# The recurrent stage of a hybrid decoder step: powers, exponentials and keys in another order

## The reference

```python
def rwkv7_scan(r, decay, k, v, kk, kka, s0):
    def step(s, inp):
        r_t, w_t, k_t, v_t, kk_t, kka_t = inp
        s_kk = jnp.einsum('bhvk,bhk->bhv', s, kk_t)
        s = s * w_t[:, :, None, :] - s_kk[..., None] * kka_t[:, :, None, :] + v_t[..., None] * k_t[:, :, None, :]
        return s, jnp.einsum('bhvk,bhk->bhv', s, r_t)
...
    w_log = -jax.nn.softplus(-(w0 + jnp.tanh(zw) @ w2).astype(f32)) - 0.5
    decay = jnp.exp(-jnp.exp(w_log))
    a = jax.nn.sigmoid((a0 + za @ a2).astype(f32))
...
    kk = k * ph(k_k)
    kk = kk / jnp.maximum(jnp.sqrt(jnp.sum(kk * kk, axis=-1, keepdims=True)), 1e-12)
    k = k * (1.0 + (a - 1.0) * ph(k_a))
    y, s_final = rwkv7_scan(r, decay, k, v, kk, kk * a, s0.astype(f32))
```

## Time and profile before

| what | value |
|---|---|
| median of 3 runs | 3446.24 us (3445.89 to 3452.47) |
| profiled execution, its own time | 3446.67 us |
| its span, first to last instruction | 3445.1 us |
| mean granted TensorE clock | 0.952 |
| TensorE matmuls busy | 3162.6 us (92%) |
| VectorE busy | 2162.1 us (63%) |
| ScalarE busy | 1105.0 us (32%) |
| GpSimd busy | 521.5 us (15%) |

### The profile page before, as it was taken

The page is one execution under the profiler, slowest core; times in us unless marked ns, Lnnn a source line. Parts: engine busy times, 40 slices in busy tenths (PEclk is TensorE's granted clock), DMA queues, the critical chain, the costliest instruction groups (busy, mean ns, idle before and its releaser), DMA issues. The chain is left out here.

```text
span 3445.1 us, 66198 instructions
## 1 busy us (share of the span) xinstructions
PE 3162.6 (92%) x25784; PEld 1917.1 (56%) x25784; DVE 2162.1 (63%) x4342; ACT 1105.0 (32%) x2313; POOL 521.5 (15%) x732
## 2 busy tenths in 40 slices
PE   8999999999999999869999865877876999999998
PEld 4544445555555555446666544777765555555553
DVE  2017889999999999658776554677772444432221
ACT  4135660000000000135555324677762211111221
POOL 3331000000000000021111132455542000000000
PEclk9999999999999999979999976889897999999999
DMA  5232111111111111132111181222215211221110
GB/s 161 72 93 66 43 41 57 56 55 58 55 57 62 55 58 55 59 96 67 43 44 33 49 271 47 57 62 66 64 31 158 100 52 54 64 78 58 49 40 25
DMA packets 215817, 233.54 MB, mean 68 GB/s; under 512 B 28665, under 2 KB 191028, under 8 KB 215012
## 3 DMA queue, kind: packets, MB, share of 16 engines
q1 hardware_dynamic: 147960, 110.07, 11.8%
q0 software_dynamic: 23696, 59.79, 6.0%
q10 hardware_dynamic: 43868, 59.62, 5.0%
HBM read 158.75 MB, written 70.63 MB: 67 GB/s over the span
## 5 line engine op out<-in xcount | busy, mean ns | idle before, releaser
L409 PE MATMUL fro_acc<-h_t,fro_w 128*128 128x416 f32 x3280 | 1174.6, 516 | 0.0
L409 PEld LDWEIGHTS fro_acc<-h_t,fro_w 128*128 128x128 f32 x3280 | 614.5, 190 | 543.1 <-issue 536.1
L692 DVE TENSOR_SCALAR_CACHE_REDUCE fro_work<-scores,fro_real 128x384 uint8<-128x384 f32 (+6 forms) x462 | 656.2, 1474 | 2.1
L516 ACT ACTIVATE fro_out<-fro_acc 128x416 f32<-128x416 f32 (+3 forms) x230 | 118.0, 513 | 794.1 <-PE fro_acc L409 711.6
L3105 DVE CUSTOM_DVE_ANT_0 att_seen<-att_ps,scores 128x512 f32<-128x512 f32 (+3 forms) x320 | 181.4, 608 | 99.8 <-PE att_ps L2991 99.5
L2169 PE MATMUL mrg_po<-mrg_wo,mrg_mrg 128*128 128x512 f32 (+1 forms) x544 | 238.8, 597 | 4.6 <-DVE mrg_mrg L2274 4.6
L2201 PE MATMUL mrg_pg<-mrg_wg,mrg_x_t 128*128 128x512 f32 (+1 forms) x544 | 236.3, 592 | 0.0
L658 DVE SCALAR_TENSOR_TENSOR scores<-fro_work,w_idx,scores 128x512 f32<-128x512 f32 (+3 forms) x280 | 188.0, 671 | 39.2 <-ACT fro_work L573 12.2
L3075 ACT ACTIVATE att_seen<-att_seen,att_shift 128x128 f32<-128x128 f32 (+15 forms) x128 | 152.6, 1194 | 83.2 <-DVE att_shift L3113 83.2
L2169 PEld LDWEIGHTS mrg_po<-mrg_wo,mrg_mrg 128*128 128x128 f32 (+1 forms) x544 | 101.5, 187 | 139.1 <-issue 134.1
L573 ACT ACTIVATE fro_work<-fro_wk 128x512 f32<-128x512 f32 (+3 forms) x320 | 144.5, 540 | 90.7 <-PE fro_wk L482 89.8
(11 more groups left out here) (449 smaller groups left out, 4523.5 us busy)
## 6 DMA issues: line engine op xcount, KB each, us to landing
z_t<-fro_out ACTq DMA_DIRECT2D x180, 208.0 KB
fro_w<-in_w_in SPq DMA_DIRECT2D x41, 512.0 KB, 4.1
mrg_m_in<-z_t POOLq DMA_DIRECT2D x56, 256.0 KB, 3.5
scores<-in_cache_kv POOLq DMA_DIRECT2D x108, 128.0 KB, 3.1
rwk_zi<-z_t SPq DMA_DIRECT2D x80, 129.0 KB, 2.6
z_t<-fro_out ACTq DMA_DIRECT2D x45, 192.0 KB
scores<-in_x_prompt SPq DMA_DIRECT2D x16, 512.0 KB, 8.4
mrg_x<-in_x_prompt SPq DMA_DIRECT2D x16, 512.0 KB, 3.5
```

Source lines behind the costliest of these rows:

```text
L409: last = pe.matmul(acc[e % 2][:, 0:CW], w[block_no % 3][:, kk, :], h_t[:, kk, CW * g:CW * g + CW], start=(kk == 0), stop=(kk == KD - 1))
L692: chain.mark(dve.tensor_scalar(junk[b % 2][:, 0:n], scores[:, c:c + n], realf[:, b:b + 1], None, op, ALU.add, accum_out=count[:, b:b + 1]))
```

## The change

Only the order of calls inside a round changes, on three engines. No instruction is added or taken away, and GpSimd's and SyncE's lists stay as they are.

```diff
@@ TensorE
                 if inverse:
                     square(n + 1, 2)
-                if features:
-                    norms(n + 2)
                 if loop:
                     take_in(n, 1)
                 if inverse:
                     square(n + 1, 3)
+                if features:
+                    norms(n + 2)
+                if inverse:
                     turn_rates(n + 1)
@@ ScalarE
                 if norm:
                     deviation(n - 1)
+                if inverse:
+                    take_square(n + 1, 1)
                 if features:
                     exps(n + 2)
+                if inverse:
+                    take_keys(n + 1)
+                    take_square(n + 1, 2)
+                if features:
                     spread_norms(n + 2)
                     take_values(n + 2)
-                if inverse:
-                    take_square(n + 1, 1)
-                    take_keys(n + 1)
-                if features:
                     key_mix(n + 2)
-                if inverse:
-                    take_square(n + 1, 2)
@@ VectorE
                 if loop:
                     next_state(n, 1)
+                if inverse:
+                    power(n + 1, 3)
                 if features:
                     unit_key(n + 2)
                     mixed_key(n + 2)
-                if inverse:
-                    power(n + 1, 3)
                 if inputs:
                     add_parts(n + 3, 1)
-                if features:
-                    scaled_keys(n + 2)
                 if inverse:
                     power(n + 1, 4)
                 if features:
+                    scaled_keys(n + 2)
                     scaled_rows(n + 2)
```

## The result

| | median | range | runs |
|---|---|---|---|
| before | 3449.22 us | 3445.89 to 3452.47 | 4 |
| after | 3501.53 us | 3499.45 to 3514.28 | 4 |

The ratio is 1.016 with a 95% interval of 1.014 to 1.0181: 52 us slower, where 35 were forecast. The direction was right, the time lies 7.5 us above the end of the range. The profiled execution of the changed kernel took 3514.28 us, 13 more than its median and 67.6 more than the profiled one before. Of these 67.6 us, 55.9 lie in rounds 0 to 12 of the recurrent stage, 3.9 in its other rounds, and 7.8 outside the stage, where the two kernels are the same. So part of the 13 us is scatter of other stages.

What follows compares the result with a forecast made beforehand. The recurrent stage was taken as bound by a chain from engine to engine, no engine full. Longer rounds 28.3, other rounds 0.7 and tail clock 6.5 made 35.5 us on 3446.67, giving 3481 us, range 3460 to 3494.

Steps and rivals of the forecast that it cites:

- Edit 1, the cancellation: ScalarE's second-power copy ahead of the exponentials: 2.25 us earlier, but the third-power copy starts when it does today.
- Edit 2, the inputs later: VectorE's unit and mixed keys behind power 3: next inputs (L1740) end 1.40 us later, round 31.59 us.
- the collision: VectorE's L1739 beside GpSimd's L1204: the stretching moves to L1740 or L1204, -0.2 to +0.3 us a round.
- Edit 3: VectorE's scaled keys behind power 4: 1.14 us out of power 4's way, gain covered; costs nothing by 0.3 us.
- Size (a), square 1 slow in five rounds: TensorE's square 1 at the 1.2 GHz level in five of 13 rounds: 0.83 us more in those, mean 31.91.
- Size (b), the clock in the tail: TensorE at the lower clock behind new idle late in the round: 1.0 us in half the rounds, bounds 0 and 1.0.
- The path: ScalarE's squash of the next inputs (L1525): whatever moves it moves the round, 4.85 us before the next.
- the bonus arm: GpSimd's product, then TensorE's bonus sums and side: side ready at 2391.6, wanted by ScalarE only at 2393.38.
- The other rounds: The filling round and round 13 of the recurrent stage: together 0.7 us more, bounds -1.4 and +1.4.
- TensorE's faster square 2: Rival: square 2 at full clock without its idle, round's end following TensorE: 10 us less, 3436; 7 in 100.
- the tail had no give: Rival denied here: 1.4 to 2 us of give in ScalarE's tail absorbs the later L1740, 3440 to 3453; 7 in 100.

Runs made afterwards that it cites:

- Edit 1 alone: Kernel before with only ScalarE's second power copied ahead of the exponentials and the third ahead of norms, values and key mix: 3444.93 us, ratio 0.9978.
- the filled hole: Kernel before with ScalarE copying values and spreading norms while square 1 runs, then copying the second power, then the exponentials: 3430.19 us, ratio 0.9935.
- edit 2 alone: Kernel before with only VectorE's power 3 moved ahead of the unit and mixed keys: 3530.83 us, ratio 1.0235.
- The filled gaps: Changed kernel with 4 extra TensorE matmuls ahead of square 4 and 16 ahead of the bonus sums, results unused: 3480.19 us, ratio 1.008.

## Why the forecast was right in kind and short in size

- **Edit 1, the cancellation: right.** Behind square 1's copy there are 8.41 us to the last power copy (8.48 forecast), with no idle. Edit 1 alone gave 6 us, close to nothing, and the filled hole bears the reading out: with 0.99 us less behind the copy, the 13 rounds became 1.34 us shorter each.
- **Edit 2, the inputs later: right, size by the collision short.** From power 3's transpose to the end of L1741 are 4.68 us, 4.24 forecast. The collision moved to L1741 as the text said it might, but costs 0.44 and not the 0.3 that was the upper end: L1740 takes 0.62 less, and L1741 1.07 more (1.75 against 0.68 alone).
- **Edit 3: right alone, not within the change.** Alone it is zero. With edit 2 alone the side square waits 1.34 us a round for the flip, a wait that the changed kernel doesn't have.
- **Size (a), square 1 slow in five rounds: wrong, too high.** It took 1.10 us in all 13 rounds, and the copy behind it starts 13.5 to 13.6 us behind the first copy in rounds 4, 8 and 11 alike. Its 0.32 us a round did not come.
- **Size (b), the clock in the tail: the step that failed.** I took 1.0 us in half the rounds, thus 6.5 us in all, with 1.0 as the upper bound. Measured: from L1526 to the next round 2467.34 - 2461.02 = 6.32 us against 4.85, **1.47 a round, and in rounds 4 and 11 as in round 8**, thus 19 us in 13 rounds. The bonus sums ran at the lower level in 11 of the 13 rounds, the key sums in all. The 1.47 are 0.33 by which the corner starts later behind the squash, 0.33 in the corner itself and 0.81 in the key sums. I had taken 1.0 for the first two together, more than the 0.66 they cost, and left out the key sums, which went from 0.99 to 1.80 us (from their start to that of the next round). And I had let the lower level end with the round. It goes on into the beginning of the next one (0.54 in the window above), where square 1 then starts 13.20 us into the round instead of the 12.43 of round 7: 0.77 more, or 10 us in 13 rounds, for which the sum had nothing.
- **The path, the other step that failed.** I had written that whatever moves L1525 moves the round. With the tail at the lower clock that no longer holds: TensorE works without idle from the bonus sums at 2460.49 to the next round, and with the inputs ahead of the keys the squash came 2.4 us earlier on the mean while the rounds got 1.2 us longer. I had the bonus arm in view, at full clock with edit 3 and as part of the 1.0 us with the clock, but not as the arm that leads. The direction came out right all the same, because both arms hang on edit 2.
- The sum of round 8: 31.59 + 0.77 + 0.44 + 1.47 - 0.07 (8.41 for 8.48) = 34.20, measured 34.21. It is a sum along the squash, and right as one; since TensorE ends the round, it does not say that the round would be 0.44 us shorter without the collision.
- **The other rounds, and the range.** For the rounds outside the 13 I took 0.7 us, 1.4 at most on either side; in the profile they are 3.9 us longer. And the range to 3494 left out two bounds of my own, 0.3 us a round for the collision and 1.4 for those rounds; with them it would have reached 3500, still short of 3501.5.
- The filled gaps are close to the rest of the sum: without the tail's clock term it was 28.3 + 0.7 = 29.0 us more than before, and 3480.19 - 3450.89 are 29.3, with a mean round of 31.95 (31.91 forecast). The agreement is in part luck: the sum holds 4.2 us for a slow square 1, the extra matmuls have a price of their own, and the collision adds to it.
- The rivals: nothing followed TensorE's faster square 2, and the tail had no give.

## What to carry to other kernels

In a loop whose engines take turns, moving a link earlier helps only if the work behind it on the same engine shrinks; count what the engine still has to do up to the next link that others wait for, and fill the hole that the move opens. Before putting "late" work behind a wait, ask who is waited for through it: here two producers, the keys and the inputs, stood ahead of a link and filled VectorE's wait for it, and behind the link they cost 46 of the 52 us. Then look again at which arm ends the loop, since it need not be the one that ended it before. And when an order opens a gap in TensorE, look in the trace how far the lower clock reaches: here it was the whole end of the round and part of the next, and not the rows next to the gap alone.

## What the runs showed of the hardware

- An idle TensorE can be dearer than a busy one: 20 extra matmuls a round made the changed kernel 21 us faster (3501.5 to 3480.2), and raised the granted clock of the stage from 0.79 to 0.96. The same matmuls cost 43 us in the kernel before.
- The same TensorE rows, from the bonus sums to the next round, took 6.85 us without idle behind a gap of 2.54 us (clock 0.50 at the end of that round) and 3.9 to 4.1 us with the gap filled (1.00).
- A VectorE `tensor_tensor` with two SBUF inputs of 128x512 took 1.75 us beside a GpSimd `tensor_tensor`, and 0.68 without one beside it. The stretched one begins 0.17 us after GpSimd's has (2459.23 and 2459.06); the one directly ahead of it (L1740, 2458.90) begins 0.16 before and got through in 0.42, and GpSimd's took 1.37 instead of 1.27. It is so in 14 of the 16 rounds.
- The key sums, a group of eight matmul rows that give two columns each, went from 0.99 to 1.80 us at the lower level: nearly the whole factor of two, though each gives so few columns.
